# The opening of a transformer block on one core: sums of squares in order of arrival, the first tile in parts, two copies on ScalarE, one ada group later

## The reference

```python
def rmsnorm(x, g):
    y = xf * lax.rsqrt(jnp.mean(xf * xf, axis=-1, keepdims=True) + RMS_EPS)
    return y * g
...
m = jax.nn.silu(cvec) @ w_ada_l + b_ada_l          # shift1, scale1, gate1, shift2, scale2, gate2
h = rmsnorm(x, g_attn) * (1 + scale1) + shift1
u = h @ w_in_l                                     # q, k, v of two mixers, and the gates
```

## Time and profile before

| | |
|---|---|
| median of 3 runs | 889.26 us (888.52 to 889.55) |
| span of the profiled execution | 885.9 us |
| PE busy | 875.5 us (99%) |
| PE weight loads busy | 833.5 us (94%) |
| VectorE busy | 707.4 us (80%) |
| ScalarE busy | 468.5 us (53%) |
| read from and written to HBM | 121.68 MB, 12.20 MB |

### The profile page before, as it was taken

The page is one execution under the profiler, slowest core; times in us unless marked ns, Lnnn a source line. Parts: engine busy times, 40 slices in busy tenths (PEclk is TensorE's granted clock), DMA queues, the critical chain, the costliest instruction groups (busy, mean ns, idle before and its releaser), DMA issues. The chain is left out here.

```text
span 885.9 us, 16547 instructions
## 1 busy us (share of the span) xinstructions
PE 875.5 (99%) x6227; PEld 833.5 (94%) x6227; DVE 707.4 (80%) x1333; ACT 468.5 (53%) x976; POOL 122.3 (14%) x155
## 2 busy tenths in 40 slices
PE   7999999999999999999999999999999999999998
PEld 5788888898989999999999999999999999999997
DVE  5567898899788499774777879997778898777987
ACT  6663444777777533432256645555535555545553
POOL 0000000010000000000000042322433322333221
PEclk9999999999999999999999999999999999999999
DMA  9964343541543220237307299868989887899867
GB/s 367 369 221 172 131 141 120 167 126 53 171 149 108 73 72 1 79 113 322 129 24 238 63 196 203 177 166 210 200 192 203 178 187 165 197 207 189 183 150 148
DMA packets 51664, 145.32 MB, mean 164 GB/s; under 512 B 6001, under 2 KB 12417, under 8 KB 50177
## 3 DMA queue, kind: packets, MB, share of 16 engines
q1 hardware_dynamic: 32000, 102.38, 35.1%
q0 software_dynamic: 18864, 41.11, 24.2%
q10 hardware_dynamic: 720, 0.77, 0.2%
HBM read 121.68 MB, written 12.20 MB: 151 GB/s over the span
## 5 line engine op out<-in xcount | busy, mean ns | idle before, releaser
L1334 ACT ACTIVATE w_hi<-stage 128x512 fp32r<-128x512 f32 (+1 forms) x186 | 106.0, 608 | 91.5 <-DMA stage<-stage 45.8
L2034 DVE TENSOR_TENSOR w_lo<-stage,w_hi 128x512 fp32r<-128x512 f32 (+1 forms) x186 | 117.8, 668 | 20.3 <-ACT w_hi L1334 19.9
L2651 PE MATMUL ps<-m_hi,w_hi 128*128 128x320 f32 x304 | 93.9, 309 | 0.0
L2651 PE MATMUL ps<-m_lo,w_hi 128*128 128x320 f32 x304 | 93.9, 309 | 0.0
L2651 PE MATMUL ps<-m_hi,w_lo 128*128 128x320 f32 x304 | 93.9, 309 | 0.0
L1429 DVE TENSOR_TENSOR w_lo<-stage,w_hi 128x1024 fp32r<-128x1024 f32 x47 | 57.2, 1221 | 35.7 <-ACT w_hi L888 35.4
L2651 PE MATMUL ps<-h_hi,w_hi 128*128 128x320 f32 x272 | 84.1, 309 | 0.0
L2651 PE MATMUL ps<-h_hi,w_lo 128*128 128x320 f32 x272 | 84.1, 309 | 0.0
L2651 PE MATMUL ps<-h_lo,w_hi 128*128 128x320 f32 x272 | 84.0, 309 | 0.0
L2651 PE MATMUL ps<-y_hi,w_hi 128*128 128x320 f32 x264 | 81.7, 309 | 0.0
L2651 PE MATMUL ps<-y_hi,w_lo 128*128 128x320 f32 x264 | 81.6, 309 | 0.0
(11 more groups left out here) (320 smaller groups left out, 2440.6 us busy)
## 6 DMA issues: line engine op xcount, KB each, us to landing
stage<-w_main SPq DMA_DIRECT2D x118, 512.0 KB, 4.2
x<-w_ada SPq DMA_DIRECT2D x21, 512.0 KB, 4.6
stage<-stage POOLq DMA_DIRECT2D x38, 256.0 KB, 4.4
qk<-w_ada SPq DMA_DIRECT2D x7, 1024.0 KB, 14.3
scr<-w_main POOLq DMA_DIRECT2D x28, 256.0 KB, 6.0
y_t<-scr POOLq DMA_DIRECT2D x22, 320.0 KB, 6.7
s_second<-w_main POOLq DMA_DIRECT2D x26, 256.0 KB, 5.9
stage<-w_main POOLq DMA_DIRECT2D x19, 256.0 KB, 6.7
```

Source lines behind the costliest of these rows:

```text
L1334: act.activation(w_hi[:, slot, at:at + job_half(j) * P], left_stage(op, j), ACT.Copy).then_inc(left_hi[op], 1)
L2034: dve.tensor_tensor(w_lo[:, slot, w], left_stage(op, j), w_hi[:, slot, w].bitcast(F32), ALU.subtract).then_inc(left_lo[op], 1)
L2651: ins = pe.matmul(ps[:, BANK_OF[op], 0:TH], wt[:, slot, w], right(op, part, j, k), start=k == 0 and n == 0, stop=k == half - 1 and n == 2)
```

## The change

- ScalarE squares the tiles in the order 0, 2, 4, 1, 5, 3, 6, 7, and VectorE adds in that order: five adds into sq[0], and sq[6] + sq[7] by itself. PE sums the columns of both into the same PSUM cells: ten products in place of five.
- The two silu rows are copied out of PSUM by ScalarE, behind the squares, not by VectorE.
- The identity matmuls on PE are gone.
- xn[0] is made in the three parts of H_PARTS. PE broadcasts the inverse roots of each part by itself (`root_columns`), into banks 6, 7 and 4, with ada columns 0 behind the first; `rbc` is copied behind part 2.
- Weight unit 0 is split in two halves of 512 columns on both engines, the second behind part 2 of h. PE starts once the first half is there, and needs the second for tile 1.
- Ada group 2 on PE stands in front of bank i = 0 of tile 0, behind banks 1, 2, 4 and 3, not ahead of the whole tile; it waits for `rbc`. ScalarE's copy of its row stays ahead of the split of unit 1 and of `h_tile(1)`.
- Two semaphores are merged into pool_set, and counts that others wait for are renumbered (left out below).

```diff
--- before.py
+++ after.py
...
@@ -585,6 +586,8 @@
+        X_ORDER = (0, 2, 4, 1, 5, 3, 6, 7)
         def load_x(eng, k):
@@ -691,7 +694,7 @@
                 if a < ADA2_SLOTS:
-                    sp.wait_ge(xn_done, KT)
+                    sp.wait_ge(xn_done, KT + 2)
                 else:
@@ -889,7 +892,7 @@
-                act.wait_ge(xn_done, n + 1)
+                act.wait_ge(xn_done, n + 3)
                 if n % KT >= 2:
@@ -917,15 +920,24 @@
                 load_x(act, k)
-            act.wait_ge(pool_set, 1)
+            act.wait_ge(pool_set, 2)
             act.activation(small[:, 53:54], eps, ACT.Tanh)
...
             act.activation(small[:, 52:53], eps, ACT.Sqrt)
-            for k in range(KT):
+            for k in X_ORDER:
                 act.wait_ge(x_in[k], 16)
                 act.activation(sq[k], x[:, k * T:(k + 1) * T], ACT.Square).then_inc(sq_done, 1)
+            for v, bank in ((0, 0), (1, 4)):
+                act.wait_ge(cbc_ready, v + 1)
+                act.activation(cbc[:, v * D_MODEL:(v + 1) * D_MODEL].rearrange("p (a b) -> p a b", a=2),
+                               ps[:, bank:bank + 2, :], ACT.Copy).then_inc(cbc_copied, 1)
+            def first_unit_hi(half, done):
+                w = slice(half * 512, (half + 1) * 512)
+                act.activation(w_hi[:, 0, w], stage[:, 0, w], ACT.Copy).then_inc(done, 1)
@@ -933,20 +945,24 @@
-            split_hi(0, 0)
             act.wait_ge(rms_ss, 1)
...
             copy_ada(0)
-            act.wait_ge(xn_done, 1)
-            act.activation(rbc[:, 0:T], ps[:, 6:8, :].rearrange("p a b -> p (a b)")[:, 0:T], ACT.Copy).then_inc(rbc_done, 1)
+            act.wait_ge(stage_in[0], 16)
+            first_unit_hi(0, first_hi)
             for k in range(KT):
...
                     copy_ada(1)
+                    act.wait_ge(xn_done, 2)
                     h_first_part(1)
+                    act.wait_ge(xn_done, 3)
+                    act.activation(rbc[:, P:T].rearrange("p (a b) -> p a b", a=2), ps[:, 6:8, 0:2 * P], ACT.Copy)
+                    act.activation(rbc[:, 0:P], ps[:, 4, 0:P], ACT.Copy).then_inc(rbc_done, 1)
                     h_first_part(2)
+                    first_unit_hi(1, hi_done)
                 else:
@@ -1250,7 +1266,7 @@
             def spread(half):
-                act.wait_ge(rms_bc, 2 + half)
+                act.wait_ge(rms_bc, 4 + half)
                 act.activation(rbc[:, half * TH:(half + 1) * TH], ps[:, 2 + half, 0:TH], ACT.Copy).then_inc(rbc_done, 1)
@@ -1447,29 +1463,24 @@
             dve.wait_ge(c_tanh, 1)
-            dve.wait_ge(cpad_zero, 1)
+            dve.wait_ge(pool_set, 1)
             own.mark(dve.scalar_tensor_tensor(out=csilu[:, 2 * KT:4 * KT], in0=csilu[:, 2 * KT:4 * KT], scalar=1.0,
...
                               ALU.mult).then_inc(c_ready, 1)
-            def copy_cbc(v):
-                dve.wait_ge(cbc_ready, v + 1)
-                bank = (0, 4)[v]
-                dve.tensor_copy(cbc[:, v * D_MODEL:(v + 1) * D_MODEL].rearrange("p (a b) -> p a b", a=2),
-                                ps[:, bank:bank + 2, :]).then_inc(cbc_copied, 1)
-            for k in range(1, KT):
-                dve.wait_ge(sq_done, k + 1)
-                if k > 1:
-                    dve.wait_ge(sum_done, k - 1)
-                dve.tensor_tensor(sq[0], sq[0], sq[k], ALU.add).then_inc(sum_done, 1)
+            for n in range(1, 6):
+                dve.wait_ge(sq_done, n + 1)
+                if n > 1:
+                    dve.wait_ge(sum_done, n - 1)
+                dve.tensor_tensor(sq[0], sq[0], sq[X_ORDER[n]], ALU.add).then_inc(sum_done, 1)
+            dve.wait_ge(sq_done, KT)
+            dve.tensor_tensor(sq[6], sq[6], sq[7], ALU.add).then_inc(sum_done, 1)
             dve.wait_ge(consts_in, 16)
...
             own.wait()
-            copy_cbc(0)
@@ -1505,17 +1516,28 @@
             dve.reciprocal(rms_r, rms_sd).then_inc(rms_rec, 1)
-            copy_cbc(1)
-            dve.wait_ge(rms_bc, 1)
-            dve.tensor_tensor(xn[0], x[:, 0:T], ps[:, 6:8, :].rearrange("p a b -> p (a b)")[:, 0:T], ALU.mult).then_inc(xn_done, 1)
+            def x_first_part(i):
+                t = H_PARTS[i]
+                dve.wait_ge(rms_bc, i + 1)
+                dve.tensor_tensor(xn[0][:, t], x[:, t], ps[:, (6, 7, 4)[i], 0:t.stop - t.start], ALU.mult).then_inc(xn_done, 1)
+            def first_unit_lo(half, hi, done):
+                w = slice(half * 512, (half + 1) * 512)
+                dve.wait_ge(hi, 1)
+                dve.tensor_tensor(w_lo[:, 0, w], stage[:, 0, w], w_hi[:, 0, w].bitcast(F32), ALU.subtract).then_inc(done, 1)
+            x_first_part(0)
             modulation(0)
-            split_lo(0, 0)
+            first_unit_lo(0, first_hi, first_lo)
+            x_first_part(1)
             h_first_low(0)
+            x_first_part(2)
+            h_first_low(1)
             dve.wait_ge(rbc_done, 1)
             x_scaled(1, 1, whole)
-            h_first_low(1)
             h_first_low(2)
             modulation(1)
+            first_unit_lo(1, hi_done, lo_done)
             split_lo(1, 1)
@@ -2236,10 +2258,8 @@
                     pe.wait_ge(mod1, k - 1)
-                elif k == 3:
+                elif k >= 2:
                     pe.wait_ge(rbc_done, 1)
-                elif k == 2:
-                    pe.wait_ge(cbc_copied, 2)
                 st = ada1_st[k % ADA1_SLOTS]
@@ -2265,31 +2285,33 @@
             silu_row(1)
-            def keep_clock(k, n):
-                pe.wait_ge(sum_done, k)
-                pe.matmul(ps[:, 6, 0:n], ident, x[:, k * T:k * T + n], start=True, stop=True)
-            for k, n in ((2, 512), (4, 512), (5, 512), (6, 256)):
-                keep_clock(k, n)
-            pe.wait_ge(sum_done, KT - 1)
-            for c in range(5):
-                ins = pe.matmul(ps[:, 7, c:c + 1], sq[0][:, c * P:(c + 1) * P], one1, start=True, stop=True)
-            ins.then_inc(rms_ss, 1)
+            def sum_columns(tile, last):
+                for c in range(5):
+                    ins = pe.matmul(ps[:, 7, c:c + 1], tile[:, c * P:(c + 1) * P], one1, start=not last and c == 0,
+                                    stop=last and c == 4)
+                return ins
+            def root_columns(i):
+                t = H_PARTS[i]
+                for n, c in enumerate(range(t.start // P, t.stop // P)):
+                    ins = pe.matmul(ps[:, (6, 7, 4)[i], n * P:(n + 1) * P], rms_r[:, c:c + 1].to_broadcast([P, P]), ident,
+                                    start=True, stop=True)
+                ins.then_inc(rms_bc, 1)
+            pe.wait_ge(sum_done, 5)
+            sum_columns(sq[0], False)
+            pe.wait_ge(sum_done, 6)
+            sum_columns(sq[6], True).then_inc(rms_ss, 1)
             ada_groups(0)
             pe.wait_ge(rms_rec, 1)
-            for c in range(5):
-                ins = pe.matmul(ps[:, 6 + c // 4, c % 4 * P:(c % 4 + 1) * P], rms_r[:, c:c + 1].to_broadcast([P, P]), ident,
-                                start=True, stop=True)
-            ins.then_inc(rms_bc, 1)
-            def keep_clock_late(n):
-                pe.matmul(ps[:, 5, 0:n], ident, x[:, 0:n], start=True, stop=True)
+            root_columns(0)
             ada_columns(0)
+            root_columns(1)
+            pe.wait_ge(cbc_copied, 2)
+            root_columns(2)
             ada_groups(1)
-            pe.wait_ge(cbc_copied, 2)
-            keep_clock_late(256)
-            ada_groups(2)
@@ -2311,14 +2333,20 @@
                     pe.wait_ge(h_ready, k + 3)
-                if k % 2 == 0:
+                if k == 0:
+                    pe.wait_ge(first_lo, 1)
+                elif k == 1:
+                    pe.wait_ge(lo_done, 1)
+                elif k % 2 == 0:
                     pe.wait_ge(lo_done, k // 2 + 1)
...
                         ada_columns(1)
+                    elif i == 0:
+                        ada_groups(2)
                     pe.wait_ge(*((h_ready, 3), (h_ready, 1), (h_ready, 1), (h_ready, 2), (h_ready, 2))[i])
-                    pe.wait_ge(*((mod1, 2), (cbc_copied, 1), (cbc_copied, 1), (mod1, 2), (cbc_copied, 2))[i])
+                    pe.wait_ge(*((mod1, 2), (cbc_copied, 1), (cbc_copied, 1), (mod1, 1), (cbc_copied, 2))[i])
@@ -2429,7 +2457,7 @@
                     pe.wait_ge(v_in, 16 * 3)
-                    pe.wait_ge(pool_set, 2)
+                    pe.wait_ge(pool_set, 4)
                 for c in range(len(parts[0])):
```

More of the change, by code:

```diff
@@ L428, in hybrid_dit_program @@
         c_ready = sem("c_ready")
-        cpad_zero, cbc_copied = sem("cpad_zero"), sem("cbc_copied")
+        cbc_copied = sem("cbc_copied")
         ada_pe, ada_copied, ada_t = sem("ada_pe"), sem("ada_copied"), sem("ada_t")
@@ L436, in hybrid_dit_program @@
         x1_done, sum2_done, first_half = sem("x1_done"), sem("sum2_done"), sem("first_half")
+        first_hi, first_lo = sem("first_hi"), sem("first_lo")
```

(8 more changed lines are left out.)

## The result

| | before | after |
|---|---|---|
| median of 10 runs each | 889.52 us | 892.86 us |
| lowest to highest | 887.40 to 891.09 | 890.26 to 894.16 |
| span of the profiled execution | 885.9 us | 890.0 us |
| TensorE's mean granted clock in it | 0.999 | 0.995 |
| first projection matmul (T0) | 21.0 us | 20.6 us |

The changed kernel is slower by a ratio of 1.0037 (95% interval 1.0027 to 1.0047), 3.3 us. The forecast was 889.9, the range ended at 892.0. The profile after names the place at once. First the windows of the changed kernel; the columns are the stretch, its length, busy time and instructions of PE, PEld, DVE, ACT and POOL, then the granted clock, the DMA share and GB/s.

A forecast was written before the change was run, and what follows sets the result against it. TensorE, busy 99% of the span, was taken as the bound. The first projection would come 2.5 us earlier, but ScalarE's queue would start tile 1 0.65 us later: 889.26 + 0.65 = 889.9 us, range 888.4 to 892.0.

The forecast's parts named there:

- ada group 0 starts: On PE behind the column sums: start at about 14.25 us instead of 15.53, 1.3 us gained.
- silu copies on ScalarE, each: Two 128x1024 copies out of PSUM, 1.0 us each from 11.3 to 13.4, hidden and costing nothing.
- T0 at a full clock: First projection matmul on PE at 18.5 us, 2.5 us earlier.
- ScalarE idle before the copy of row 2: ScalarE idle for 1 to 1.5 us before copying ada row 2, released by PE's ada group.
- K1 at a full clock: PE's first matmul of tile 1 (k = 1) at 27.1 us against 26.45, 0.65 us later.
- K1 when group 2 alone is moved: Start of tile 1: group 2 ends 4.43 us after the first projection, then 4.11 more; 29.6 us expected.
- the queue: ScalarE's in-order wait for group 2 delays ada row 2's copy, weight unit 1 and h tile 1: 0.65 us later.
- (c): Rival: ScalarE's queue doesn't hold tile 1, which starts at PE's own 25.3 us; 888.1 us total; chance 0.08.
- tile to tile afterwards: After tile 1 starts, later tiles on PE follow every 5.0 us.
- The clock: PE's opening without filler: price shown by no row, nothing in the sum; a fall to half rate left to rivals.
- rival (a): Clock falls in the opening: first projection 20.0, tile 1 at 28.6, 891.4 us, up to 892.5; chance 0.26.
- (b): Rival: clock falls in the 1.8 us hole before tile 1, whose matmuls cost +1.7 us; 891.6 us; chance 0.14.

The follow-up runs named there:

- experiment 3: Changed kernel with column sums on PE streaming 96 copies of the ones column instead of one: 889.57 us against 888.86 before, ratio 1.0011.
- experiments 2: Kernel before, identity matmuls kept, with only ada group 2 moved in front of bank i = 0 of tile 0: 892.65 us against 888.86, ratio 1.0045.
- experiments 5: Changed kernel with 96-column sums and h tile 1 first on ScalarE, run twice: ratios to the kernel before 0.9987 (887.79 us) and 0.9985 (887.32 us).
- experiment 4: Changed kernel with ScalarE making h tile 1 before copying ada row 2 and splitting weight unit 1: 889.56 us against 888.86 before, ratio 1.0009.
- experiment 7: Changed kernel with 96-column sums and h tile 1 first, silu copies put back on VectorE: 888.27 us against 888.89 before, ratio 0.9996.
- Experiment 1: Kernel before without its identity matmuls, nothing else changed: 891.96 us against 888.86, ratio 1.0035.
- experiment 6: Changed kernel with 96-column sums and two 512-column identity matmuls ahead of k = 1: 890.46 us against 889.10 before, ratio 1.0011.
- experiment 8: Changed kernel with 96-column sums and h tile 1 first, old square order and one set of sums: 891.42 us against 888.89 before, ratio 1.0027.

## Why the prediction was wrong

**The sum was right, the likeliest case was not.** Every step up to K1 can be read off the kernels that kept their clock in the opening, or off a stretch that the low clock didn't touch:

| step | forecast | measured |
|---|---|---|
| ada group 0 starts | 14.25 | 14.20 (after) |
| silu copies on ScalarE, each | 1.0 us | 1.92 us for both (after) |
| T0 at a full clock | 18.5 | 18.6 (experiment 3) |
| ScalarE idle before the copy of row 2 | 1 to 1.5 | 1.52 (3), 1.75 (after) |
| K1 at a full clock | 27.1 | 27.2 (3) |
| K1 when group 2 alone is moved | T0 + 8.6 | T0 + 8.65 (2) |
| K1 without the queue, (c) | 25.3 | 25.5 and 25.85 (5) |
| tile to tile afterwards | 5.0 | 4.96 (after) |

K1 came 3.31 us later than before (29.76 against 26.45). Of these, 0.76 are the queue, forecast at 0.65: K1 at a kept clock was 27.21. The other 2.55 are the low clock of the opening, which the sum had at nothing.

**The step that failed is "The clock".** The prediction gave rival (a) 0.26 and (b) 0.14, on the ground that PE's queue is never empty for more than 0.5 us. That ground failed twice. First, it was not so: PE was idle for 1.44 us ahead of the sums in the changed kernel, because the silu rows came up to speed sooner and were done at 10.43; the prediction took their end, 11.4, from one execution of the kernel before. Second, it wasn't what decided: in experiment 4 the idle time was 0.58 us and the clock fell during the narrow sums, in experiments 5 and 7 it was 1.16 and 1.22 and the clock held behind wide ones. Passes that stream a single column behind a weight load count as busy in the profile (2.39 us for the twenty), and in these kernels the clock fell behind them. The hint was in the rows: ten such passes take 1.28 us in the earlier trace rows and stream ten columns in all, and the filler in front of them streamed 256 or 512 in every pass. Experiment 1 gives the price that no row showed: 3.1 us in the median for the filler alone.

**Rival (a)'s own price was too small.** It charged half clock to the end of the sums and to group 0 (T0 20.0, K1 28.6), 1.5 us over the forecast K1 of 27.1; measured are 2.55. In the trace the clock fell only at about 15 but stayed low to about 21.7: group 1 took 1.94 in place of 1.07, the root columns of part 0 1.22 in place of 0.71 (experiment 3), ada columns 0.85 in place of 0.61, and the first projection matmuls were slow too. T0 became 20.6 and K1 29.76. Group 1, hidden at a full clock, became the bound of T0: the first projection follows it on PE without idle time, where experiment 3 has 0.3 us. From T0 to K1 it then took 9.2 us in place of 8.6, because the low clock lasted on past T0.

**Rival (b) is real as well.** It didn't strike in the profiled execution of the changed kernel, and did in those of experiments 2 and 3, at a cost of 1.6 us each; with the hole filled (experiment 6) one of eleven executions was at 0.998 and none below, where experiment 3 had five of twelve at 0.998 or less. The low clocks of 0.993 among the ten executions leave room for both in one, which no trace shows.

**The range** ended at 892.0, with 891.4 as the price of (a). The two errors, a chance too low and a price too small, both pushed the same way. Slower by over 0.2% had 0.28; it was the outcome.

**The rule of the Trainium skill** ("TensorE: Matmul & The Clock Gate", part 1: the array is held at half rate unless activity releases it) was weighed and left as a rival. The traces agree with it: behind 3.3 us without a matmul the granted clock was 0.59 from 15 to 19 us (experiment 1) and 0.50 from 18 to 22 (experiment 8), and with wide sums the stretch from 15.0 to 21.7 had 1.00 where the changed kernel had 0.50 (experiment 3).

## What to carry to other kernels

Before filler matmuls are taken out, look at what TensorE streams in their place, and not only at whether the profile calls it busy: here 2.4 us of weight-bound passes of one column had the clock falling in most executions, and widening them to 96 columns kept it there, for 0.1 us more. Don't count on the idle time of one trace either: ahead of the sums it was 0.1 to 1.4 us over the traces of the new order. When work is moved back in one engine's queue, follow the first in-order consumer of its result and everything queued behind that consumer: here one copy of 0.38 us carried a whole tile, and making that tile first brought K1 from 27.2 to 25.5. A gain at the first matmul (2.5 us at T0 in the forecast) is no gain until the next point where the engines meet has it too.

## What the runs showed of the hardware

The profile's granted clock begins with its first change. The clock column says 1.00 from the start in both kernels; only the durations tell when the silu passes came up to speed (421 and 275 ns in the earlier trace rows); the 32 passes took 6.28 us in the kernel before and 5.18 in the changed one, so the rise comes at another time in another execution.

A low clock lasts differently long. It was 6.7 us in the changed kernel and 10.1 in experiment 4, though PE was busy in every microsecond of it, and some 3.3 us in experiments 1, 2 and 3 (0.59 over 4.0 us and 0.62 over 4.5 are 3.3 and 3.4 us at half speed; in experiment 3 the matmuls are slow from 27.9 to 31.3). The kind of work behind the fall doesn't explain it by itself: in experiment 1 the clock came back among root columns and ada columns, in experiments 2 and 3 the low clock lasted as long among dense 512-column matmuls. What decides it stays open here.

Executions of one kernel differ by 2 to 3 us for two reasons that the traces show. A second trace of the kernel before has T0 at 21.8 and K1 at 27.3, 0.8 us later than the first and than expected, since the squares and with them the chained adds came later (PE then waited 0.7 and 0.2 us for them):

> The kernel before, unchanged, for a second trace. First projection at 21.0 and k = 1 at 26.4 to 26.5. The five other traces have one more wait at about 531 us of the trace of before, of 0.4 to 0.8 us, where PE waits for a weight split in the feed-forward. If that is the drift of transfers from one execution to the next, this trace has it or not as it comes; if a later opening caused it, this trace doesn't have it.

```profile
PE ps L2651 <- DVE w_lo L2034: 1.0, 1, 1.0
PE ps L2270 <- DVE scr L1466: 0.7, 1, 0.7
...
PE ps L2277 <- DVE scr L1466: 0.2, 1, 0.2
```

And at 531 us, where the feed-forward's weight splits begin to depend on sums made by transfers, PE waits for VectorE's w_lo for anything from nothing to 1.8 us, as the profile has it: nothing in the first trace of before and in experiment 7, 1.0 in the second of before, 0.6 in the changed kernel, 1.8 in experiment 6. The kernel before has it in one trace and not in the other, so it can't be put down to an edit, and nothing says that the 0.8 us that the changed kernel's trace loses there are the change's. The 885.9 us of the first trace was a lucky execution: the second has 887.9, and the spans of the 71 executions beside the experiments lie at 885.4 to 888.9.
